# Compressed q normed between the last products of its stage, and the work for compressed kv and the rotary key placed beside the first heads of q

## What is computed

```python
qkv, z, beta_lg, decay_lg, cq, ckv, k_rope, gates = _split_in(h @ w_in[l])
...
q = (_rms(cq, q_a_norm) @ w_uq).reshape(B, T, MLA_HEADS, MLA_QK)
kv = (_rms(ckv, kv_a_norm) @ w_ukv).reshape(B, T, MLA_HEADS, MLA_NOPE + MLA_V)
k_nope, v = kv[..., :MLA_NOPE], kv[..., MLA_NOPE:]
k = jnp.concatenate([k_nope, jnp.broadcast_to(k_rope[:, :, None, :], (B, T, MLA_HEADS, MLA_ROPE))], axis=-1)
q = _rms(q, q_norm)
k = _rms(k, k_norm)
```

## Time and profile before

| | |
|---|---|
| median of three runs | 2790.85 us |
| profiled execution | 2791.21 us |
| its span, first to last instruction | 2789.4 us |
| mean granted TensorE clock | 0.968 of full speed |
| busy, share of the span | PE 93%, DVE 59%, POOL 41%, ACT 23% |
| read from HBM, written | 224.91 MB, 2.17 MB |

### The profile page before, as it was taken

One profiled execution on the slowest core, in us unless ns is written; L12 is line 12 of the kernel. 1 busy time (PEld: TensorE's weight loads), 2 busy tenths in 40 slices (PEclk: granted clock), 3 DMA queues, 4 the chain that ended last, 5 costly groups with the idle time before them and its releaser, 6 DMA issues. The chain is left out here.

```text
span 2789.4 us, 45359 instructions
## 1 busy us (share of the span) xinstructions
PE 2587.0 (93%) x18586; PEld 2157.7 (77%) x18586; DVE 1644.3 (59%) x2509; ACT 632.7 (23%) x1231; POOL 1149.0 (41%) x930
## 2 busy tenths in 40 slices
PE   8989999989889999989899989978798999899998
PEld 6778888778567888868788878864686888688887
DVE  7948758472658838667564656533576515563451
ACT  4221112110322101133443244301354100110000
POOL 3535545454134454424431433111332545455453
PEclk9989999999999999989899999989999999999999
DMA  4223343222024334211011101101200222222322
GB/s 156 92 105 138 123 146 134 86 92 89 1 76 151 140 119 155 100 60 65 25 41 47 61 27 39 47 29 31 48 24 31 91 91 101 80 91 91 101 95 75
DMA packets 51316, 229.68 MB, mean 82 GB/s; under 512 B 5296, under 2 KB 12480, under 8 KB 32576
## 3 DMA queue, kind: packets, MB, share of 16 engines
q1 hardware_dynamic: 51136, 227.10, 23.4%
HBM read 224.91 MB, written 2.17 MB: 81 GB/s over the span
## 5 line engine op out<-in xcount | busy, mean ns | idle before, releaser
L246 POOL TENSOR_TENSOR ring_rounded<-ring,ring_rounded 128x512 fp32r<-128x512 f32 (+2 forms) x715 | 934.7, 1338 | 1146.7 <-DVE ring_rounded L237 1134.1
L286 PE MATMUL psum<-arena_rounded,ring_rounded 128*128 128x512 f32 (+1 forms) x2820 | 1100.3, 390 | 62.8 <-PEq L515 13.8
L287 PE MATMUL psum<-arena_rounded,ring_rounded 128*128 128x512 f32 (+1 forms) x2820 | 1091.2, 387 | 0.0
L288 PE MATMUL psum<-arena_rounded,ring_rounded 128*128 128x512 f32 (+1 forms) x2820 | 1089.8, 386 | 0.0
L286 PEld LDWEIGHTS psum<-arena_rounded,ring_rounded 128*128 128x128 f32 x2820 | 536.5, 190 | 184.2 <-issue 47.6
L288 PEld LDWEIGHTS psum<-arena_rounded,ring_rounded 128*128 128x128 f32 x2820 | 536.2, 190 | 107.6
L287 PEld LDWEIGHTS psum<-arena_rounded,ring_rounded 128*128 128x128 f32 x2820 | 536.5, 190 | 104.3 <-issue 1.5
L237 DVE CAST ring_rounded<-ring 128x2048 fp32r<-128x2048 f32 (+4 forms) x191 | 212.3, 1112 | 677.1 <-PE psum L288 618.3
L713 ACT ACTIVATE arena<-psum,vectors 128x512 f32<-128x512 f32 x88 | 68.5, 781 | 409.1 <-PE psum L288 409.1
L329 DVE TENSOR_TENSOR arena_rounded<-arena,arena_rounded 128x512 fp32r<-128x512 f32 (+2 forms) x113 | 125.3, 1108 | 3.9
L327 DVE CAST arena_rounded<-arena 128x512 fp32r<-128x512 f32 (+2 forms) x113 | 114.0, 1009 | 9.3 <-DVE arena L743 1.0
(11 more groups left out here) (408 smaller groups left out, 3039.4 us busy)
## 6 DMA issues: line engine op xcount, KB each, us to landing
ring<-in_w_up SPq DMA_DIRECT2D x44, 1024.0 KB, 4.8
arena<-in_w_mod SPq DMA_DIRECT2D x48, 512.0 KB, 3.4
ring<-in_w_down SPq DMA_DIRECT2D x32, 704.0 KB, 4.0
ring<-in_w_mup SPq DMA_DIRECT2D x16, 1024.0 KB, 4.8
ring<-in_w_mdown SPq DMA_DIRECT2D x16, 1024.0 KB, 4.8
ring<-in_w_gdn SPq DMA_DIRECT2D x12, 1024.0 KB, 4.8
ring<-in_w_lru_in SPq DMA_DIRECT2D x10, 1024.0 KB, 4.9
ring<-in_w_odd_in SPq DMA_DIRECT2D x10, 1024.0 KB, 4.7
```

The source lines that it names most:

```text
L246: last = pool.tensor_tensor(self.rounded(low), raw, self.rounded(high).bitcast(F32), ALU.subtract)
L286: pe.matmul(out, r(wh), r(xh), start=start, stop=False)
L287: pe.matmul(out, r(wh), r(xl), start=False, stop=False)
L288: return pe.matmul(out, r(wl), r(xh), start=False, stop=stop)
```

## The change

In `mla_in_stage` the last unit's products are written out in four blocks (first tile, 512 and 256 columns; second tile, the same). Behind the first block TensorE takes the column sums for q, behind the second it spreads q's four roots. DVE makes the mean, the Newton step and the three norms of q before it takes the last unit out; with this the stage ends. What compressed kv and the rotary key need goes into `mla_heads_stage`: the squares of the second kv tile and of the key, and later the high parts of kv, on ACT; the sums behind unit 0, the spread behind unit 2 and the rotation of the key behind unit 3 on TensorE; the add, the mean, the Newton step, the key's gain, the scaled products, the key's turn and the low parts on DVE ahead of units 0 to 5; the power on POOL between two low parts. Unit 6 waits for both kv blocks (`lready`), the first turn of q for the key's (`krturned`). The scratch places move so that they outlive the stage. Names of the rows and sums change with it: the sums and the mean now come from the helpers at L335 and L341.

```diff
     def pe(pe):
-        for unit in us:
-            if unit.u == 2:
-                pe.wait_ge(m.sem("freed"), m.count("freed", 2))
-            pe_wide_unit(m, pe, unit, lambda k: (xh[:, k, :], xl[:, k, :]), wide[2 * unit.u:2 * unit.u + 2],
-                         unit.u == 0)
-        pe.wait_ge(m.sem("summed"), m.count("summed", 3))
-        for i in range(4):
-            pe.matmul(m.psum[:, 7, i:i + 1], accs[0][:, i * P:(i + 1) * P], m.ones[:, 0:1], start=True, stop=True)
-        for i in range(NA):
-            last = pe.matmul(m.psum[:, 7, 4 + i:5 + i], accs[1][:, i * P:(i + 1) * P], m.ones[:, 0:1],
-                             start=True, stop=True)
-        last.then_inc(m.up("ssq"), 1)
-        pe.wait_ge(m.sem("loaded"), m.count("loaded", 16 * len(loads)))
-        pe.wait_ge(m.sem("krgain"), m.count("krgain", 1))
-        pe.matmul(m.psum[:, 0, :], m.at(ROT_AT, P), kr[:, 0:T], start=True, stop=True).then_inc(m.up("rotated"), 1)
-        pe.wait_ge(m.sem("rstd"), m.count("rstd", 1))
-        rstd_pe_spread(m, pe, root, 4, lambda i: m.psum[:, 6, i * P:(i + 1) * P])
-        rstd_pe_spread(m, pe, root[:, 4:10], 6, lambda i: m.psum[:, 4 + i // 4, (i % 4) * P:(i % 4 + 1) * P])
+        halves = lambda k: (xh[:, k, :], xl[:, k, :])
+        for unit in us[:2]:
+            pe_wide_unit(m, pe, unit, halves, wide[2 * unit.u:2 * unit.u + 2], unit.u == 0)
+        last = us[2]
+        pe.wait_ge(m.sem("freed"), m.count("freed", 2))
+        pe.wait_ge(m.lo_done, last.g + 1)
+        for t in range(2):
+            for i, cols in enumerate((slice(0, T), CTX)):
+                out = m.psum[:, 4 + last.slot, t * TC:(t + 1) * TC] if i else m.psum[:, 2 * last.slot + t, :]
+                for k in range(KD):
+                    o = k * seg.cols + t * P
+                    w = [m.ring[:, part, last.slot, o:o + P] for part in (1, 2)]
+                    ins = m.product(pe, out, w, [x[:, cols] for x in halves(k)], k == 0, k == KD - 1)
+                if (t, i) == (0, 0):
+                    pe.wait_ge(m.sem("summed"), m.count("summed", 2))
+                    rstd_pe_sums(m, pe, qacc, NT, 7)
+                if (t, i) == (0, 1):
+                    ins.then_inc(m.up("done"), 1)
+                    pe.wait_ge(m.sem("rstd"), m.count("rstd", 1))
+                    rstd_pe_spread(m, pe, root, NT, lambda i: m.psum[:, 6, i * P:(i + 1) * P])
+        ins.then_inc(m.up("done"), 1)
...
-        for t in range(6):
-            act.wait_ge(m.sem("freed"), m.count("freed", t + 1))
-            n = TA if wide[t] else T
-            dst = {0: accs[0], 3: accs[1], 5: krsq}.get(t, sq[:, t % 2, 0:n])
-            act.activation(dst, outs[t], ACT.Square).then_inc(m.up("square"), 1)
+        for n in range(4):
+            act.wait_ge(m.sem("freed"), m.count("freed", n + 1))
+            dst = {0: qacc, 3: kvacc}.get(n, sq[:, n % 2, 0:T])
+            act.activation(dst, outs[n], ACT.Square).then_inc(m.up("square"), 1)
...
-        for unit in us:
+
+        def evict(unit):
...
+        dve.memset(half, -0.5).then_inc(m.up("half"), 1)
+        split_xn(m, dve, xh, xl)
+        evict(us[0])
+        add(1)
+        evict(us[1])
+        add(2)
         dve.wait_ge(m.sem("ssq"), m.count("ssq", 1))
...
+        rstd_dve_mean(m, dve, m.psum[:, 7, 0:NT], mean, 1.0 / 384)
         dve.wait_ge(m.sem("root"), m.count("root", 1))
         rstd_newton(m, dve, mean, root, tmp, m.sig("rstd"))
-        dve.wait_ge(m.sem("spread"), m.count("spread", 2))
+        dve.wait_ge(m.sem("spread"), m.count("spread", 1))
         for k in range(3):
...
-        for k in range(2):
...
-            split_in_place(m, dve, ckh[:, k, :], ckl[:, k, :], m.sig("lready"))
+        evict(us[2])
...
-        rstd_pool(m, pool, mean, half, root, 1)
+        pool.wait_ge(m.sem("half"), m.count("half", 1))
+        rstd_pool(m, pool, mean, half[:, 0:NT], root, 1)
...
+        def kv_sums():
+            pe.wait_ge(m.sem("kvsummed"), m.count("kvsummed", 1))
+            rstd_pe_sums(m, pe, kvacc, NA, 6, "kvssq")
+
+        def kv_spread():
+            pe.wait_ge(m.sem("kvrstd"), m.count("kvrstd", 1))
+            rstd_pe_spread(m, pe, kvroot, NA, lambda i: m.psum[:, 4 + i // 4, (i % 4) * P:(i % 4 + 1) * P])
+
+        def key_turn():
+            pe.wait_ge(m.sem("krgain"), m.count("krgain", 1))
+            pe.wait_ge(m.sem("kvmean"), m.count("kvmean", 1))
+            pe.matmul(m.psum[:, 6, :], m.at(ROT_AT, P), kr[:, 0:T], start=True, stop=True).then_inc(
+                m.up("krrotated"), 1)
+
...
+                if n == 6:
+                    pe.wait_ge(m.sem("lready"), m.count("lready", 2))
                 pe_wide_unit(m, pe, unit, khalves, [True] * 2)
...
+            if n == 0:
+                kv_sums()
+            if n == 2:
+                kv_spread()
+            if n == 3:
+                key_turn()
...
+        act.activation(kvsq, ckl[:, 1, :], ACT.Square).then_inc(m.up("kvsquare"), 1)
+        act.activation(krsq, kr, ACT.Square).then_inc(m.up("krsquare"), 1)
         for n, unit in enumerate(us[:10]):
+            if n in (4, 5):
+                k = n - 4
+                act.wait_ge(m.sem("kvnormed"), m.count("kvnormed", k + 1))
+                act.activation(m.rounded(ckh[:, k, :]), ckl[:, k, :], ACT.Copy).then_inc(m.up("kvhigh"), 1)
...
+        def kv_normed(k):
+            if k == 0:
+                dve.wait_ge(m.sem("spread"), m.count("spread", 1))
...
+                ins = dve.scalar_tensor_tensor(o, o, col(v["kv_a_norm"], k), m.psum[:, b, 0:o.shape[1]],
+                                               ALU.mult, ALU.mult)
...
+        def kv_low(k):
+            dve.wait_ge(m.sem("kvhigh"), m.count("kvhigh", k + 1))
+            dve.wait_ge(m.sem("kvnormed"), m.count("kvnormed", k + 1))
+            low = ckl[:, k, :]
+            dve.tensor_tensor(m.rounded(low), low, m.rounded(ckh[:, k, :]).bitcast(F32), ALU.subtract).then_inc(
+                m.up("lready"), 1)
...
+        def key_turned():
+            x = kr[:, 0:T]
+            dve.wait_ge(m.sem("krrotated"), m.count("krrotated", 1))
+            dve.tensor_tensor(rot, m.at(SIN_AT, T), m.psum[:, 6, :], ALU.mult).then_inc(m.up("krturned"), 1)
+            dve.tensor_tensor(x, x, m.at(COS_AT, T), ALU.mult).then_inc(c.up(), 1)
...
+            dve.tensor_tensor(x, x, rot, ALU.add).then_inc(c.up(), 1)
...
         m.dve_kept(dve)
+        dve.wait_ge(m.sem("kvsquare"), m.count("kvsquare", 1))
+        dve.tensor_tensor(kvacc, kvacc, kvsq, ALU.add).then_inc(m.up("kvsummed"), 1)
         for n, unit in enumerate(us):
+            if n == 1:
+                dve.wait_ge(m.sem("kvssq"), m.count("kvssq", 1))
+                dve.tensor_scalar(kvmean, m.psum[:, 6, 0:NA], 1.0 / 256, EPS, ALU.mult, ALU.add).then_inc(
+                    m.up("kvmean"), 1)
+            if n == 2:
+                dve.wait_ge(m.sem("kvroot"), m.count("kvroot", 1))
+                dve.wait_ge(m.sem("kvmean"), m.count("kvmean", 1))
+                rstd_newton(m, dve, kvmean, kvroot, kvtmp, m.sig("kvrstd"))
+                dve.wait_ge(m.sem("krsquare"), m.count("krsquare", 1))
+                dve.tensor_scalar(kr, kr, v["k_norm_rope"], None, ALU.mult).then_inc(m.up("krgain"), 1)
+            if n == 3:
+                kv_normed(0)
+                kv_normed(1)
+            if n == 4:
+                dve.wait_ge(m.sem("krgain"), m.count("krgain", 1))
+                key_turned()
+            if n == 5:
+                kv_low(0)
+                kv_low(1)
             dve.wait_ge(m.sem("done"), m.count("done", 2 * n + 2))
...
-        for unit in us:
+        m.pool_unit(pool, us[0])
+        pool.wait_ge(m.sem("kvmean"), m.count("kvmean", 1))
+        pool.tensor_tensor(kvroot, kvmean, kvhalf, ALU.pow).then_inc(m.up("kvroot"), 1)
+        for unit in us[1:]:
             m.pool_unit(pool, unit)
```

More of the change, by code:

```diff
@@ L2589 @@
 KRS_AT, PR_AT, PT_AT = 12288, 15360, 16896
+KV_ACC_AT, KV_SQ_AT = XN_AT + T, XN_AT + T + TA
+KV_HALF = slice(54, 60)
 def mla_in_stage(m, seg, v, loads):
@@ L2595, in mla_in_stage @@
     cqh, cql = m.at(CQ_AT, 3, T), m.at(CQ_AT + 3 * T, 3, T)
-    ckh, ckl = m.at(CKV_AT, 2, TA), m.at(CKV_AT + 2 * TA, 2, TA)
-    kr, krsq = m.at(KR_AT, TA), m.at(KROW_AT, TA)
-    accs = [m.at(XN_AT, T), m.at(XN_AT + T, TA)]
-    sq = m.at(XN_AT + T + TA, 2, TA)
-    rot = m.at(XN_AT + T + 3 * TA, T)
+    ckl = m.at(CKV_AT + 2 * TA, 2, TA)
+    kr = m.at(KR_AT, TA)
+    qacc, kvacc, sq = m.at(XN_AT, T), m.at(KV_ACC_AT, TA), m.at(KV_SQ_AT, 2, TA)
     outs = [cql[:, 0, :], cql[:, 1, :], cql[:, 2, :], ckl[:, 0, :], ckl[:, 1, :], kr]
     wide = [False] * 3 + [True] * 3
-    mean, root, tmp, half = [m.small[:, 24 + 10 * i:34 + 10 * i] for i in range(4)]
+    mean, root, tmp = [m.small[:, a:a + NT] for a in (24, 34, 44)]
+    half = m.small[:, KV_HALF]
     us = unrolled(seg)
@@ L2655, in dve @@
                 ins.then_inc(m.up("freed"), 1)
-            for t in range(2):
-                n = 2 * unit.u + t
```

(7 more changed lines are left out.)

41 lines of the change are left out of this document (20 added, 21 removed).

## The result

The changed kernel takes 2768.96 us, the median of four runs (2766.81 to 2770.53), against 2790.91 us for the kernel before in the same comparison: a ratio of 0.9922, 95% interval 0.9905 to 0.9939, 22 us less. 2770 us was forecast, with a range of 2766 to 2775. The profiled execution took 2766.81 us, its span is 2765.0 us, its mean granted clock 0.97 of full speed.

A forecast was written before the change was run, and what follows sets the result against it. TensorE, busy 93% of the span, was taken as the bound, so its standstills count. From 2791.21 us profiled, -24.0 + 3.9 - 0.7 = -20.8 gives 2770.4; the median, 0.36 lower, gives 2770 us, range 2766 to 2775.

The forecast's parts named there:

- The hole: Between input and heads stages: 28.2 us without big products, set by DVE's chain and barrier; heads start 24.0 us earlier.
- the gap: Behind the input stage's last product: four evictions 1.94 us, a start of 0.04 and the barrier 0.32, together 2.3 us.
- No wait for the root: Input stage's last unit: q's root is done before PE reaches the spread at 1831.2, with 0.5 us to spare.
- rival B: Input stage: root comes late, PE waits before the spread; 2 us late gives 2772; counted within the forecast's 84%.
- TensorE's passes in the heads: Between q's units in the heads: every added pass counts in full, sums 1.5, spreads 1.3, turned key 1.1, together 3.9 us.
- DVE at nothing: Heads units 0 to 5: 8.9 us of moved DVE work costs nothing, covered by 21 us of idle time.
- rival A: Heads: DVE's cover is too thin, moved work shows in full, 2779 to 2781 us (half exposed 2775); 12%.
- Beside POOL: Heads: each of five moved two-input DVE steps may take 0.5 us more beside POOL, 2.5 in all, inside the cover.
- The clock: Heads' start: 3.4 us at half speed after the 2.3 us gap, 1.7 lost instead of 2.4; gain 0.7 us.
- the first of the two rows: Earlier stage start at 786.27: after 2.24 us without PE work, 3.4 us at half speed; the other row kept 1.00.
- rival C: Heads' start: small f32 passes among the products hold PE at half clock up to the turns, 2806 us; 2%.

The follow-up runs named there:

- The two single parts: Kernel before with only q's root chain and norms moved: 2784.59 us; with only compressed kv's chain and the key's turn moved: 2777.72 us.
- eight spreads: Changed kernel with the spread of kv's root done 8 times over, 84 passes more on TensorE: 2782.71 us.
- four additions: Changed kernel with 4 unused 128x512 additions more on DVE in each of heads units 1 to 5: 2778.51 us.
- The short gaps: Changed kernel with unread products in the gap, 2774.33 us; with the last unit evicted in parts, 2771.13; with that and q's rotary units first, 2759.20.
- The later comparisons: Changed kernel, unedited, run again in two more sittings, each with the kernel before: 2774.83 and 2774.05 us.
- the additions: Changed kernel with 4 or 8 unused 128x512 additions more on DVE in each of heads units 1 to 5: 2778.51 and 2789.55 us.
- rotary units first: Changed kernel with q's two rotary units ahead of the other four, each half turned one or more units after its eviction: 2761.03 us.
- the filler: Changed kernel with 9 unread 128x128 f32 products on TensorE after the input stage's last product: 2774.33 us.

## Why the prediction was right

**The hole.** The forecast of -24.0 us for the heads' start was -24.1 us. Its terms: sums 1.0, measured 0.94; spread 0.9, measured 1.05; both together lengthen the unit by 1.8; the gap 2.3, measured 2.31, and made of what was named, evictions and barrier. The two single parts show that the reason holds and not only the sum: the same adding up gave 18.5 and 11.7 us for their holes, and 19.6 and 11.7 came out.

**No wait for the root** (rival B): PE came to the spread with 0.66 us to spare, 0.5 was forecast. B is out, though by a small margin.

**TensorE's passes in the heads, +3.9 us.** The rows are 1.39 + 1.50 + 1.02 = 3.9. The forecast had 1.5, 1.3 and 1.1, so three small misses cancel; the spread was the one taken too low, in both stages, since half of its time at half clock (0.11 a pass) left out that a short group of passes takes longer than its share (1.05 us for 8, 1.50 for 12, against 10.88 for 96). The eight spreads show that such passes count in full.

**DVE at nothing.** The work was sized well (8.9 us forecast; DVE's busy time from H to A rose by 8.6), and the conclusion was right, since PE has no wait from H to the turns, but the step behind it was wrong. The prediction took the idle time ahead of evictions and weight roundings, 4.2 us a unit and 21 us in all, as the cover. The chain mean, power, Newton, spread has its own due time at PE, and there the spare was 1.36 us. Had the last Newton row come 1.4 us later, rival A would have begun, and that it did not is in part luck: nothing in the prediction had looked at this margin. It would then have cost by its excess, as with four additions, not the full length that A was priced at.

**Beside POOL.** DVE's add of kv's squares, two inputs in SBUF, took 1.61 us at 1841.22 where the same shape takes 0.96 (1865.58 in the earlier trace rows), and POOL's two low parts from 1841.00 on took 2.69 us together, where the next two took 1.99. Both engines lost 0.65 to 0.70 us, once; the forecast had allowed 0.5 us at each of five steps.

```profile
1841.00 2.69 POOL L246 TENSOR_TENSOR ring_rounded<-ring,ring_rounded 128x384 fp32r<-128x384 f32 x2 [13.81 <-DVE ring_rounded L237]
```

That fits the Trainium skill, "SBUF — State Buffer", "Who interferes with whom", by which such instructions of the two exclude each other. The times are near those of taking turns: POOL's first piece ends at 1842.01, the add, 0.96 us long by itself, 0.82 us behind it at 1842.83, and POOL's second piece, 1.73 us long where the first took 1.01, 0.87 us behind the add. It was hidden here, as costed.

**The clock.** 3.4 us at half clock was assumed and 3.4 came. That the first of the two rows would hold and not the second was a choice without a reason in the rows beyond the barrier, and the seventh profile with this gap went the other way; it would have moved the sum by 1.7 us. From H to A the change costs 2.6 to 3.1 us in three profiles, against 3.9 - 0.7 = 3.2. The short gaps, all at full clock, speak for the gap as the right cause to look at. Nothing of rival C was seen: 37 us at full clock with the helper passes among the products.

**What the median owes to chance.** -22.0 us against -20.8. The later comparisons gave -20.0 and -22.2. Of the profiled run's 24.4 us, 2.4 lie ahead of the last unit, where no work of TensorE was moved, and 1.4 of these are the clock behind S. Why executions of the same instructions reach the input stage at different times was not looked into and stays open.

## What to carry to other kernels

Where a stage ends in a chain of small steps, ask of each step which products it really needs: what needs only early tiles can be normed beside the last ones, and what nobody reads until later can go into the next stage; the gain of each is its own length, and the price is its passes on the engine that is the bound. Count the cover of a moved chain at the place where the bound engine takes its result, not by the idle time of the engine that carries it. And look behind the change for the next hole of the same kind: here a product that waited for the chain just ahead of it stood in every rotary unit, and taking it one or more units later gave 14 us more.

## What the hardware showed that was not expected

- A pause of 2.31 us was followed by about 3.4 us at half clock in six profiles (the changed kernel three times, the additions twice, the eight spreads; granted clock 0.57 to 0.68 over the first 4 us) and by none in a seventh, with the rotary units first. After 0.94 us (twice) and 0.30 us (once) the clock stayed at 1.00. After 3.0 us, at S, it was 0.50 to 0.63 over 4 us in seven profiles and 1.00 in six. So a pause of 2.3 to 3.0 us is a risk, not a rule.
- A clock that is kept at the start is not kept for the stage: with the filler 1.6 us were gained up to the second turn, and 0.5 to 1.1 at A. The stretches at half clock behind the turns fall differently from run to run.
